# Modulation chunks multiplied as they land, cached key tiles spread over the first four tiles, spatial weights and norm tables loaded later

## The chip, the cores and the metric

The kernel runs on one core of one Trainium2 chip. The metric is device time in microseconds, the median of three runs. TensorE (PE) multiplies and transposes, VectorE (DVE) and ScalarE (ACT) compute on rows, GpSimd (POOL) does small reciprocal roots here, SyncE (SP) and ScalarE issue DMA transfers. All engines run their own instruction streams in order and meet at semaphores.

## The reference, cut to what matters

One encoder layer is computed for a prompt of 1024 tokens and for a sample of 64 tokens with 512 cached frames. The change touches only the first of its parts, the one that makes queries, keys, values and gates:

```python
mod = jax.nn.silu(c) @ w_ada + b_ada                     # 1024 -> 6*1024, for both conditionings
sh_a, sc_a, gt_a, sh_m, sc_m, gt_m = split(mod, 6)
h = rms_norm(x, g_norm_mix) * (1 + sc_a) + sh_a
proj = h @ w_in                                          # q latent 256, kv latent 128, rotary 32, u 512, v 512
q = rms_norm((rms_norm(q_lat) @ w_uq).heads)             # 8 heads of 96, then rotary
k, v = split(rms_norm(ckv_all) @ w_ukv)                  # ckv_all: 512 cached rows, then the new ones
k = rms_norm(concat(k_nope, krope)) , then rotary        # also for the 4 tiles of 128 cached rows
u = gelu(g_u); v_rows = layer_norm(gelu(g_v), g_ln_v, b_ln_v)
gm = u * (w_spatial @ v_rows + b_spatial)
```

Attention, the output projection and a mixture of 32 experts follow; they are the same in both kernels.

## The kernel before, in words

The first phase goes over nine tiles of tokens: the sample (64 rows) first, then the eight prompt tiles of 128 rows. Ahead of this loop stands a startup. It multiplies silu(c) by the first third of `w_ada`, which arrives as eight chunks of 1 MiB in a ring of three buffers (`ada_w`): SP issues chunk j once PE has multiplied chunk j-3 (`s_aused`). The remaining sixteen chunks come two per tile. From the eight products come the scale and shift columns (`adaT`, `modT`, `A1`), and from them the first tile's input `hT`, half written by DVE and half by ACT.

The startup also makes keys and values of three of the four tiles of cached rows (kt 9, 10, 11; kt 12 is made within the sample's tile). One such key tile is the function `kv`: two products with `W_ukv` on PE into two PSUM banks, squares and the copy of V on ACT, and on DVE the rotary turn, sums, a root from POOL (`rstd`), and the scaling into `kh`. ACT issues their stores to `v_scratch` and `k_scratch`; those of all later key tiles are issued by SP (`store_kv`). PE also transposes the spatial weights (`wsp`) in the startup. ACT issues the loads of `wsp`, `ln_g` and `ln_b` right after its first squares.

Each tile of the loop runs, on PE: the latent projection (`lat`, 416 columns), the key tile of the tile before (`kvs`), the projection `u`, transposes of the normed latents (`latT`) and of the next tile's normed x (`xT`), the spatial product of the tile before (`mix`), the projection `gv`, the queries (`W_uq`), and two chunks of `w_ada`. On DVE: norm of the latents (`latn`), norm of the next x (`xn`), the key tile (`kv`), `latT`, the next `hT`, `mix` of the tile before, layer norm of `gv`, norm and turn of the queries, and the scaling of one eighth of `W_out`.

Seven PSUM banks are handed out in rotation: the list `order1` names every use in the order of claims with its count of readers, and a use takes the next bank. PE claims a bank by waiting until all readers of its previous use are done (`bank_freed`). So the place of a use in the list decides on whom PE waits. POOL's roots and the halves of `kh`/`vh` (two buffers, in the order `key_order`) follow the same order.

## Time and profile before

| | us |
|---|---|
| median of 3 runs | 1124.41 (1123.81 to 1124.58) |
| profiled execution | 1130.84 |
| its span, first to last instruction | 1129.1 |
| PE busy in it | 1062.4 (94%) |
| DVE busy in it | 637.2 (56%) |
| ACT busy, POOL busy | 272.5 (24%), 306.3 (27%) |
| mean granted clock of PE | 0.958 |

The page of the profile gives busy times over the whole span; the first phase is only its first 304 us. In the first of its 40 slices of 28 us PE is busy to 3 tenths, in the second to 6, in the third to 8 and then 9 or more up to the tenth slice. The DMA engines are busy to 9, 8 and 9 tenths in the first three slices. So the startup is the one stretch of this phase in which PE stands idle much, and the rows below look into it and into the steady tiles behind it. In the timelines a row is: start in us, duration in us, engine, line, operation, output<-inputs, shape, number of instructions merged into it, and in brackets the idle time ahead of it with what ended it.

### The profile page before, as it was taken

The numbers are of one execution on the slowest core, as the hardware profiler recorded it, in microseconds if no ns is written. First come the engines' busy times: TensorE is split into PE (matmuls) and PEld (weight loads), VectorE is DVE, ScalarE is ACT, GpSimd is POOL, SyncE is SP. The second block draws the span as 40 slices with busy tenths as digits, with TensorE's granted clock in tenths as the row PEclk, the third lists the DMA queues.
The fourth block names the chain that finished last, engine by engine and source line by source line (L and its number), as shares of the span: only waits on it lengthen the run. The fifth ranks groups of instructions, "written<-read, shape, count | busy, mean of one in ns | idle before, by whom it ended". The sixth has DMA issues, their size and how long they took to land.

```text
span 1129.1 us, 14437 instructions
## 1 busy us (share of the span) xinstructions
PE 1062.4 (94%) x4921; PEld 703.6 (62%) x4921; DVE 637.2 (56%) x1280; ACT 272.5 (24%) x609; POOL 306.3 (27%) x350
## 2 busy tenths in 40 slices
PE   3689999999999899999999999899999999999994
PEld 0334555555556656676777775777777777777772
DVE  1455555555556556666766678546656454544443
ACT  1243222222332223223323211221111111111110
POOL 1222222222221011110101000224534544454554
PEclk9799999999957899999999999799999999999998
DMA  9894333333344143412403029669989999898950
GB/s 310 302 373 135 142 138 133 142 143 125 126 118 107 42 112 140 159 61 99 148 30 122 20 93 368 225 236 348 355 303 344 346 352 353 336 351 331 359 197 18
DMA packets 78102, 229.80 MB, mean 204 GB/s; under 512 B 29835, under 2 KB 33566, under 8 KB 62294
## 3 DMA queue, kind: packets, MB, share of 16 engines
q1 hardware_dynamic: 50608, 198.86, 47.3%
q0 software_dynamic: 24048, 26.81, 7.1%
q10 hardware_dynamic: 3382, 3.32, 0.9%
q8 instruction: 35, 0.57, 0.2%
q14 instruction: 29, 0.24, 0.1%
HBM read 201.23 MB, written 88.25 MB: 256 GB/s over the span
## 4 chain that ended last, share of the span: by engine, by line
PE 83%; DVE 9%; DMA 2%; issue 2%; ACT 2%; POOL 1%; ACTq 1%; DVEq 0%; SPq 0%; POOLq 0%
PE bank L1033 14%; PE bank L986 10%; PE bank L1392 10%; PE bank L1394 10%; PE bank L1409 10%; PE bank L1201 9%; PE bank L1146 7%; PE bank L1171 5%; PE bank L1114 2%; PE bank L1014 2%; PE bank L998 2%; PE bank L1044 1%; DMA grope<-in_g_knorm 1%; PE bank L1223 1%; POOL st L833 1%
## 5 line engine op out<-in xcount | busy, mean ns | idle before, releaser
L1033 PE MATMUL bank<-W_in,hT 128*128 128x512 f32 (+3 forms) x480 | 172.4, 540 | 3.8 <-DMA W_in<-in_w_in 3.8
L832 POOL TENSOR_SCALAR st<-st 128x1 f32<-128x1 f32 (+5 forms) x76 | 17.5, 230 | 565.6 <-DVEq L1767 268.6
L1033 PEld LDWEIGHTS bank<-W_in,hT 128*128 128x128 f32 (+1 forms) x480 | 80.0, 185 | 91.0 <-issue 87.9
L1409 PE MATMUL bank<-WD,hidT 128*128 128x512 f32 x264 | 119.0, 594 | 1.7 <-DVE hidT L2415 1.7
L1392 PE MATMUL bank<-WG,xT 128*128 128x256 f32 x528 | 119.5, 380 | 1.0 <-DVE xT L2399 1.0
L1394 PE MATMUL bank<-WU,xT 128*128 128x256 f32 x528 | 119.4, 380 | 0.0
L1201 PE MATMUL bank<-W_out,mT 128*128 128x512 f32 (+1 forms) x288 | 114.5, 561 | 0.1
L1394 PEld LDWEIGHTS bank<-WU,xT 128*128 128x128 f32 x528 | 100.5, 190 | 13.4
L1392 PEld LDWEIGHTS bank<-WG,xT 128*128 128x128 f32 x528 | 97.9, 190 | 13.0 <-issue 1.2
L1146 PE MATMUL bank<-kT,qT 104*128 104x512 f32 (+4 forms) x224 | 92.0, 528 | 0.7 <-ACTq L1647 0.6
L1171 PEld LDWEIGHTS bank<-vall,probT 128*128 128x128 f32 (+1 forms) x656 | 79.8, 191 | 18.8 <-issue 17.3
L2188 DVE COPY probT<-bank 128x512 f32<-128x512 f32 (+3 forms) x104 | 56.9, 547 | 59.5 <-PE bank L986 52.1
L2430 DVE TENSOR_TENSOR yb<-bank,gate_w 128x512 f32<-128x512 f32 x64 | 41.2, 686 | 77.4 <-PE bank L1409 77.4
L1171 PE MATMUL bank<-vall,probT 128*128 128x64 f32 (+1 forms) x656 | 83.1, 274 | 1.0 <-DVEq L1767 1.0
L1409 PEld LDWEIGHTS bank<-WD,hidT 128*128 128x128 f32 x264 | 47.7, 190 | 49.4 <-issue 47.3
L1201 PEld LDWEIGHTS bank<-W_out,mT 128*128 128x128 f32 (+1 forms) x288 | 46.5, 183 | 46.1 <-issue 40.3
L2407 DVE TENSOR_TENSOR hid<-sg,bank 128x256 f32<-128x256 f32 x33 | 20.1, 608 | 95.2 <-ACT sg L1722 95.2
L1729 ACT ACTIVATE gate_w<-gate_m,roww 128x1024 f32<-128x1024 f32 x33 | 37.9, 1151 | 139.5 <-DVE yb L2430 135.3
L833 POOL TENSOR_TENSOR st<-st,mhalf 128x1 f32<-128x1 f32 (+5 forms) x76 | 69.4, 914 | 6.3
L904 POOL DMA_INDIRECT residual_scratch<-acc,ids x32 | 41.1, 1284 | 69.9 <-DVE acc L2436 53.0
L907 POOL DMA_INDIRECT out<-acc,ids x33 | 38.3, 1159 | 72.2 <-DMA out<-acc,ids 64.5
L1146 PEld LDWEIGHTS bank<-kT,qT 104*128 104x128 f32 (+1 forms) x224 | 38.5, 200 | 28.1 <-issue 26.4
(330 smaller groups left out, 1474.5 us busy)
## 6 DMA issues: line engine op xcount, KB each, us to landing
WG<-in_w_gate_e SPq DMA_DIRECT2D x33, 1024.0 KB, 7.1
WU<-in_w_up_e SPq DMA_DIRECT2D x33, 1024.0 KB, 9.5
WD<-in_w_down_e SPq DMA_DIRECT2D x33, 1024.0 KB, 13.0
ada_w<-in_w_ada SPq DMA_DIRECT2D x24, 1024.0 KB, 7.8
residual_scratch<-x_att SPq DMA_DIRECT2D x32, 512.0 KB, 4.4
kbuf<-k_scratch SPq DMA_DIRECT2D x12, 384.0 KB, 5.1
xbuf<-in_x_prompt SPq DMA_DIRECT2D x8, 512.0 KB, 3.7
W_in<-in_w_in SPq DMA_DIRECT2D x2, 2048.0 KB, 22.6
```

The costliest lines, as they stand in the source:

```text
L833: g.tensor_tensor(dst, dst, mhalf[:dst.shape[0], 0:dst.shape[1]], ALU.pow).then_inc(s_rs, 1)
L904: g.indirect_dma_start(z_d[group], U(idx), acc[:, k], None, bounds_check=TOK - 1, oob_is_err=False).then_inc(s_zsc[group], 16)
L986: tr = lambda out, in_, r: nc.tensor.transpose(out, in_, ident[:r, :r])
L1033: ins = mm(out, hT[:, place_of[t] % 2, k, :R], W_in[:, k, c0 + c.start:c0 + c.stop], start=(k == 0), stop=(k == KD - 1))
L1146: ins = mm(out[:R, 0:m], qT[:depth, s % 2, h, :R], kT[:depth, h, k0 + c0:k0 + c0 + m], start=True, stop=True)
L1171: ins = mm(psum[7][:R, h * VD:(h + 1) * VD], probT[:r, u % 2, b, :R], vall[:r, slot0(t) + b, h * VD:(h + 1) * VD], start=(b == 0), stop=(b ...
L1201: ins = mm(out, (mT_last if s == LAST else mT)[:, k, :R], W_out[:, k, half * 512 + c.start:half * 512 + c.stop], start=(k == 0), stop=(k = ...
L1392: mm(psum[2][:, 0:DE], xT[:, k, :], WG[u][:, k, :], start=(k == 0), stop=(k == KD - 1))
L1394: ins = mm(psum[3][:, 0:DE], xT[:, k, :], WU[u][:, k, :], start=(k == 0), stop=(k == KD - 1))
L1409: ins = mm(psum[5 + half][:], hidT[:, k, :], WD[u][:, k, half * 512:(half + 1) * 512], start=(k == 0), stop=(k == 1))
L2188: ops.append(V.tensor_copy(probT[:, u % 2, 4 * j:4 * j + len(full), :R], src[:, 0:len(full), :R]))
L2430: V.tensor_tensor(y[:, c], psum[5 + half][:], gate_w[:, par, c], ALU.mult).then_inc(s_yv, 1)
```

## The change

In the startup PE takes chunks 0 to 5 of `w_ada` with only the transpose of the vectors among them; the rotary table product and the transposes of the cached latents stand behind chunk 5 instead of chunk 2, and the sample's x transposes stay behind chunk 6. No key tile is made in the startup. The four tiles of cached rows are made at the end of the first four tiles of the loop, one each (`late_kvs`), behind the queries and ahead of the two chunks of `w_ada` on PE, and behind the query turn and ahead of the `W_out` scaling on DVE. SP issues their stores, after the store of the queries. The spatial weights are transposed by PE at the end of the sample's tile, and DVE copies them behind the sample's queries. ACT issues `ln_g`, `ln_b` and `wsp` after it has written its half of the first `hT`. The bank rotation follows the new order.

```diff
     def kvs(i):
-        return ([9 + NC_ - 1] if i == 0 else [seq[i - 1]])
-    early_keys = list(range(9, 9 + NC_ - 1))
+        return [seq[i - 1]] if i else []
+    early_keys = []
+    def late_kvs(i):
+        return [9 + i] if i < NC_ else []
...
@@ SP, in the loop over tiles
             if i < LAST:
                 store_q(i)
+            for kt in late_kvs(i):
+                store_kv(sp, kt)
@@ PE, startup
-            if j == 2:
+            if j == 5:
                 pe.wait_ge(s_grope, 16 * 7)
...
-            if j == 3:
-                pe.wait_ge(s_cT, 1)
-                pe.wait_ge(s_fold1, 2)
-                for kt in early_keys:
-                    kv(kt)
-            if j == 5:
-                pe.wait_ge(s_wspl, 16)
-                for half in range(2):
...
@@ PE, in the loop over tiles, behind the queries
+            if i == 0:
+                pe.wait_ge(s_wspl, 16)
+                for half in range(2):
...
+            for kt in late_kvs(i):
+                kv(kt)
             if i < LAST:
                 for j in loop_ada(i):
                     ada(j)
@@ ACT, startup
-        act.dma_start(wsp[:], w["w_spatial"][0].rearrange("h t s -> t h s")).then_inc(s_wspl, 16)
+        ada(0)
+        hT_half(0)
         act.dma_start(ln_g[:], bcast(w["g_ln_v"], [P, GW])).then_inc(s_params, 16)
         act.dma_start(ln_b[:], bcast(w["b_ln_v"], [P, GW])).then_inc(s_params, 16)
-        for kt in early_keys[:-1]:
+        act.dma_start(wsp[:], w["w_spatial"][0].rearrange("h t s -> t h s")).then_inc(s_wspl, 16)
...
@@ DVE, in the loop over tiles
             turn(qh[:R, :, ND:], qh[:R, :, ND:], rope_q, t if t < NT else NC_, R, H)
             signal(s_qh)
+            if i == 0:
+                spatial_weights()
+            for kt in late_kvs(i):
+                kv(kt)
             if i:
                 k = i - 1
```

PE at the start of the program, before: `ada_w` are the chunks (4 products each), `grope` the rotary gains, `cn` the normed cached latents, `latT_c` their transposes.

```order
L998 MATMUL bank<-ada_w,c_act 2x512 x8
L986 MATMUL bank<-ident,vecs 128x85
L998 MATMUL bank<-ada_w,c_act 2x512 x4
L1058 MATMUL bank<-grope,ones 128x128
L986 MATMUL bank<-ident,cn 128x128 x4
L998 MATMUL bank<-ada_w,c_act 2x512 x4
L1014 MATMUL bank<-W_ukv,latT_c 128x512 x6
L998 MATMUL bank<-ada_w,c_act 2x512 x8
L986 MATMUL bank<-ident,wsp 128x128 x8
L998 MATMUL bank<-ada_w,c_act 2x512 x4
L986 MATMUL bank<-ident,xn 128x64 x8
L998 MATMUL bank<-ada_w,c_act 2x512 x4
```

And in the changed kernel (its line numbers are 14 higher here):

```order
L1012 MATMUL bank<-ada_w,c_act 2x512 x8
L1000 MATMUL bank<-ident,vecs 128x85
L1012 MATMUL bank<-ada_w,c_act 2x512 x16
L1072 MATMUL bank<-grope,ones 128x128
L1000 MATMUL bank<-ident,cn 128x128 x4
L1012 MATMUL bank<-ada_w,c_act 2x512 x4
L1000 MATMUL bank<-ident,xn 128x64 x8
L1012 MATMUL bank<-ada_w,c_act 2x512 x4
L1000 MATMUL bank<-ident,ada_row 128x98 x4
```

The three key tiles and the eight transposes of `wsp` are gone from between the chunks.

DVE between the queries of the second prompt tile and the latents of the third, before, with what each row waits for; `bank_freed` rows wait for DVE's own last read of a bank.

```order
L1839 TENSOR_TENSOR qh<-rot,rot_90 128x8x32 [waits dve_step]
L1990 TENSOR_SCALAR W_out<-W_out,vT 128x1024 [waits dve_step]
L1787 TENSOR_SCALAR latn<-lat,st 128x256 [waits dve_step,latent_square_sums_ready,reciprocal_roots_ready]
L1788 TENSOR_SCALAR latn<-lat,st 128x128 [waits dve_step]
L1815 TENSOR_SCALAR xn<-xbuf,st 128x1024 [waits dve_step,x_square_sum_ready,reciprocal_roots_ready]
```

In the changed kernel:

```order
L1853 TENSOR_TENSOR qh<-rot,rot_90 128x8x32 [waits dve_step]
L1849 TENSOR_TENSOR rot<-cck,rope_k 128x32 [waits dve_step]
L1852 TENSOR_TENSOR rot_90<-cck,rope_k 128x16 [waits dve_step] x2
L1853 TENSOR_TENSOR krot<-rot,rot_90 128x32 [waits dve_step]
L1866 ISA ctmp,st<-cck 128x32 [waits dve_step]
L1866 ISA st 128x1
L1868 TENSOR_REDUCE st<-sq_k 128x8 [waits k_squares_and_v_ready,dve_step]
L1869 TENSOR_SCALAR st<-st 128x8 [waits dve_step]
L1876 TENSOR_TENSOR kh<-bank,st 128x4x64 [waits dve_step,bank_filled0,stored_k0,reciprocal_roots_ready]
L1876 TENSOR_TENSOR kh<-bank,st 128x4x64 [waits bank_filled1,bank_freed0]
L1878 TENSOR_TENSOR kh<-krot,st 128x8x32 [waits bank_freed1]
L2009 TENSOR_SCALAR W_out<-W_out,vT 128x1024 [waits dve_step]
```

A whole key tile now stands ahead of `latn` on DVE; the tile's own key (`lat`, not `cck`) still follows `xn`, as before. The third place is PE's claim of a bank for `gv` in the second prompt tile. Before (`latT` without `_c` is the tile's own key):

```order
L1014 MATMUL bank<-W_ukv,latT 128x512 [waits bank_freed1]
L1014 MATMUL bank<-W_ukv,latT 128x512 [waits bank_freed2]
L1033 MATMUL bank<-W_in,hT 128x512 [waits bank_freed3]
L1033 MATMUL bank<-W_in,hT 128x512 x7
L986 MATMUL bank<-ident,latn 128x128 [waits bank_freed4,latents_normed]
...
L1044 MATMUL bank<-vrows,wspT 128x64 [waits bank_freed0,v_rows_ready]
L1044 MATMUL bank<-vrows,wspT 128x64 x7
L1033 MATMUL bank<-W_in,hT 128x512 [waits bank_freed1]
```

In the changed kernel:

```order
L1028 MATMUL bank<-W_ukv,latT 128x512 [waits bank_freed4]
L1028 MATMUL bank<-W_ukv,latT 128x512 [waits bank_freed5]
L1047 MATMUL bank<-W_in,hT 128x512 [waits bank_freed6]
L1047 MATMUL bank<-W_in,hT 128x512 x7
L1000 MATMUL bank<-ident,latn 128x128 [waits bank_freed0,latents_normed]
...
L1058 MATMUL bank<-vrows,wspT 128x64 [waits bank_freed3,v_rows_ready]
L1058 MATMUL bank<-vrows,wspT 128x64 x7
L1047 MATMUL bank<-W_in,hT 128x512 [waits bank_freed4]
```

The numbers of the banks moved, the relation did not: the last row, `gv`, takes the bank of the first half of the tile's own key tile (bank 1 before, bank 4 now), which DVE frees with its first `kh`.

## Rows read from the trace of the kernel before

**Rows 1.** Timeline of PE, startup and the first tiles.

```profile
24.31 0.79 PE L1058 MATMUL bank<-grope,ones 1*128 1x128 f32 x2 [3.89 <-DMA grope<-in_g_knorm]
28.45 6.64 PE L1014 MATMUL bank<-W_ukv,latT_c 128*128 128x512 f32 x12 [0.48 <-DVEq L1767]
...
36.85 1.09 PE L986 MATMUL bank<-ident,wsp 128*128 128x128 f32 x8
...
43.13 1.89 PE L998 MATMUL bank<-ada_w,c_act 128*2 128x512 f32 x8
...
50.46 5.19 PE L1033 MATMUL bank<-W_in,hT 128*64 128x208 f32 x32 [3.81 <-DMA W_in<-in_w_in]
...
64.69 3.67 PE L1033 MATMUL bank<-W_in,hT 128*64 128x256 f32 x32
71.31 2.26 PE L1114 MATMUL bank<-W_uq,latT 128*64 128x384 f32 x8 [2.95 <-DVEq L1767]
...
76.22 5.85 PE L1033 MATMUL bank<-W_in,hT 128*128 128x416 f32 x16
```

**Rows 2.** Stretches: busy us by engine, PE's granted clock, DMA share, GB/s.

```profile
0.00:25.00 25.00, 6.69 (x27) 1.00 (x27) 2.62 (x7) 4.26 (x12) 4.67 (x19) 1.00 0.92 307
25.00:40.00 15.00, 13.82 (x61) 5.13 (x60) 7.79 (x23) 2.53 (x8) 1.93 (x2) 1.00 0.64 220
40.00:65.00 25.00, 15.85 (x99) 9.28 (x101) 10.85 (x35) 9.61 (x25) 5.55 (x8) 0.73 1.03 390
72.00:75.00 3.00, 3.00 (x14) 0.50 (x14) 1.89 (x5) 0.97 (x2) 0.63 (x2) 0.50 1.03 410
```

**Rows 3.** Timeline of DVE, startup and the sample's tile.

```profile
47.64 1.48 DVE L1824 TENSOR_SCALAR hT<-bank,A,modT 128x64 f32<-128x64 f32 x4
49.70 1.42 DVE L1892 COPY wspT<-bank 128x512 f32<-128x512 f32 x2 [0.58 <-DVE hT L1824]
...
51.92 0.19 DVE L1835 TENSOR_TENSOR rot<-cck,rope_k 128x32 f32<-128x32 f32 x1
...
69.42 1.27 DVE L1900 TENSOR_SCALAR W_uq<-W_uq,vT 128x768 f32<-128x768 f32 x2
...
73.25 0.69 DVE L1961 BATCH_NORM_STATS2 st<-gv 64x6 f32<-64x512 f32 x1
...
84.95 0.35 DVE L1787 TENSOR_SCALAR latn<-lat,st 128x256 f32<-128x256 f32 x1 [1.65 <-POOL st L833]
```

**Rows 4.** Timeline of ACT, the copy of the sample's latents.

```profile
57.94 0.70 ACT L1580 ACTIVATE lat<-bank 64x208 f32<-64x208 f32 x2 [7.24 <-DVEq L1767]
```

**Rows 5.** Timeline of DVE, from one `gv` norm to the next.

```profile
128.83 0.69 DVE L1961 BATCH_NORM_STATS2 st<-gv 128x6 f32<-128x512 f32 x1 [1.45 <-ACTq L1613]
...
139.16 0.75 DVE L1990 TENSOR_SCALAR W_out<-W_out,vT 128x1024 f32<-128x1024 f32 x1
141.17 0.35 DVE L1787 TENSOR_SCALAR latn<-lat,st 128x256 f32<-128x256 f32 x1 [1.25 <-POOL st L833]
...
143.92 0.19 DVE L1835 TENSOR_TENSOR rot<-lat,rope_k 128x32 f32<-128x32 f32 x1
...
148.15 0.88 DVE L1862 TENSOR_TENSOR kh<-bank,st 128x256 f32<-128x256 f32 x2 [2.17 <-POOL st L833]
...
149.64 0.56 DVE L1948 COPY latT<-bank 128x384 f32<-128x384 f32 x1
```

**Rows 6.** Timeline of PE, prompt tiles: a key tile, and `gv` of the first four.

```profile
92.35 7.13 PE L1033 MATMUL bank<-W_in,hT 128*128 128x512 f32 x16
...
109.51 1.88 PE L1014 MATMUL bank<-W_ukv,latT 128*128 128x512 f32 x4
...
121.03 7.09 PE L1033 MATMUL bank<-W_in,hT 128*128 128x512 f32 x16
...
149.66 7.09 PE L1033 MATMUL bank<-W_in,hT 128*128 128x512 f32 x16
...
178.64 7.06 PE L1033 MATMUL bank<-W_in,hT 128*128 128x512 f32 x16
```

More of the change, by code:

```diff
@@ L684, in store_q @@
             sp.dma_start(q_d[P * t:P * t + R], qh[:R].rearrange("p h n -> p (h n)")).then_inc(s_out1["q"], 16)
+        for kt in early_keys:
+            store_kv(sp, kt)
         for i, t in enumerate(seq):
@@ L707, in _ @@
                 store_q(i)
+            for kt in late_kvs(i):
+                store_kv(sp, kt)
         nk = 0
@@ L1063, in _ @@
                 b1.full(ins, "cT")
-            if j == 3:
-                pe.wait_ge(s_cT, 1)
-                pe.wait_ge(s_fold1, 2)
-                for kt in early_keys:
-                    kv(kt)
-            if j == 5:
-                pe.wait_ge(s_wspl, 16)
-                for half in range(2):
-                    ps = b1.claim(pe, f"wsp{half}")
-                    for i in range(4):
-                        ins = tr(ps[:, i * P:(i + 1) * P], wsp[:, 4 * half + i, :], P)
-                    b1.full(ins, f"wsp{half}")
             if j == 6:
@@ L1078, in _ @@
         adaT(0)
+        pe.wait_ge(s_cT, 1)
+        pe.wait_ge(s_fold1, 2)
+        for kt in early_keys:
+            kv(kt)
         for i, t in enumerate(seq):
@@ L1116, in _ @@
                     b1.full(ins, (f"q{half}", t))
+            if i == 0:
+                pe.wait_ge(s_wspl, 16)
+                for half in range(2):
+                    ps = b1.claim(pe, f"wsp{half}")
+                    for j in range(4):
+                        ins = tr(ps[:, j * P:(j + 1) * P], wsp[:, 4 * half + j, :], P)
+                    b1.full(ins, f"wsp{half}")
+            for kt in late_kvs(i):
+                kv(kt)
             if i < LAST:
@@ L1621, in _ @@
             act.sem_inc(s_sqq, 1)
+            for kt in late_kvs(i):
+                kv(kt)
         nk = 0
@@ L1882, in _ @@
         signal(s_fold1)
-        for kt in early_keys[:-1]:
-            kv(kt)
         ada(0)
@@ L1889, in _, with spatial_weights @@
         hT_half(0)
-        for half in range(2):
-            ps = b1.read(dve, f"wsp{half}")
-            last_read(V.tensor_copy(wspT[:, 4 * half:4 * half + 4, :], ps[:].rearrange("p (h n) -> p h n", n=P)), f"wsp{half}")
-        do(V.memset(wspT[DEC:P, :, 0:DEC], 0.0))
-        signal(s_wsp)
-        kv(early_keys[-1])
+        for kt in early_keys:
+            kv(kt)
+        def spatial_weights():
+            for half in range(2):
+                ps = b1.read(dve, f"wsp{half}")
+                last_read(V.tensor_copy(wspT[:, 4 * half:4 * half + 4, :], ps[:].rearrange("p (h n) -> p h n", n=P)), f"wsp{half}")
+            do(V.memset(wspT[DEC:P, :, 0:DEC], 0.0))
+            signal(s_wsp)
         def late_constants():
@@ L1984, in _ @@
             signal(s_qh)
+            if i == 0:
+                spatial_weights()
+            for kt in late_kvs(i):
+                kv(kt)
             if i:
```

16 lines of the change are left out of this document (7 added, 9 removed).

## The prediction, made before the result was known

> **What bounds the kernel now.** I read the page first for the share of PE, then PE's timeline for the startup, the stretches for what DMA did meanwhile, and last the timelines of DVE and PE through a steady tile. The reader is to see two regimes. Up to 50.46 us PE mostly waits: it is busy 6.69 of the first 25 us while DMA moves 307 GB/s, busy for 13.82 of the next 15 while DMA falls to 220 GB/s, and its first big product starts at 50.46 when part of `W_in` lands [rows 1, 2]. That dip is what the key tiles cost: the chunk ring holds three buffers, PE does three key tiles in 6.64 us from 28.45 on, takes no chunk meanwhile, and SP issues none. From 40 to 65 us DMA is full at 390 GB/s. In the second regime, the prompt tiles, PE runs without a gap: `gv` starts at 92.35, 121.03, 149.66 and 178.64, 28.65 us apart, the last with 0.35 of modulation transposes ahead [rows 6].
>
> The second regime has a loop that nearly binds. `gv` takes the bank of the tile's own key, which DVE frees with its first `kh`. From `gv`'s start to DVE's norm of it is 7.8 us (121.03 to 128.83). From there to the scaling of `W_out` 10.3, to `latn` 2.0 (of it 1.25 for POOL's root), to the start of the tile's key 2.75 (143.92), to the end of its first `kh` 4.7 (148.15 plus half of 0.88), and 0.1 to PE: 27.65 in all, where PE takes 28.65 [rows 5, 6]. DVE is busy for 56% of the span, yet here it is 1.0 us from setting the pace, since the loop is made of waits on POOL, ACT and PE as much as of work.
>
> **The startup.** What has to have moved before chunk 5 is there: inputs of 1.1 MB, six chunks of 1.05 MB, the rotary table and vectors 0.3, in all 7.7 MB. At the first 25 us' 307 GB/s that is 25.0 us [rows 2]. If the loads that ACT no longer issues early (1.05 MB) gave nothing back it would be 2.7 us later at 390 GB/s, 27.7. I take the middle, 26.3. The rotary gains were there at 24.31 [rows 1]. Then PE has chunk 5 (1.9), the rotary product (0.8), four transposes (at most the 1.1 of eight), chunk 6 (1.9), eight small transposes (1.1) and chunk 7 (1.9), so it ends at 35.0 [rows 1]. From chunk 7's end to `hT` it was 45.02 to 49.12 [rows 1, 3], 4.1 us, so `hT` stands at 39.3 with the semaphore. Two chunks and the latent columns of `W_in` (3.8 MB) take 9.7 us from chunk 5 on and land at 36.0: PE no longer waits for them. The sample's first product starts at 39.3 instead of 50.46, 11 us earlier. The removed key tiles, transposes, waits and stores of the startup are thereby paid out; they aren't counted again.
>
> **The sample's tile.** Two paths lead to DVE's first norm of `gv`, at 73.25 before. By DMA: the rest of `W_in`, one x tile, `W_uq` and ACT's three moved loads are 6.55 MB, 16.8 us, so `W_uq` lands at 52.8 (51.6 if chunk 5 came at 25.0), and from DVE's scaling of `W_uq` to the norm it was 69.42 to 73.25, 3.8 us [rows 3]: 56.7 or 55.5. By PE: 39.3, the latent product 5.2 at half clock as before, from ACT's copy of the latents to `gv` 57.94 to 64.69, 6.75 [rows 1, 4], then `gv` 3.7 and about 1 for the gelu: 56.0. I take 56.3, which is 16.95 earlier than before. The bounds are 54.8 (chunk 5 at 25.0 and 410 GB/s, the rate of the stretch 72 to 75 [rows 2]) and 59.5 (chunk 5 at 27.7 and 370).
>
> Behind that norm DVE has the sample's queries as before, and now also the spatial weights, 49.70 to 51.92 or 2.2 us [rows 3], and the first late key, whose length is a key tile's from start to what follows it, 143.92 to 149.64, 5.7 us [rows 5]. Only then comes `latn` of the first prompt tile, which before had 0.4 of waiting more than a steady one (1.65 against 1.25 [rows 3, 5]). So `latn`, and with it that tile's key and `gv`, move by -16.95 - 0.4 + 2.2 + 5.7 = -9.45: `gv` at 82.9. PE is there earlier: its tile ends with the queries from 55.1 (2.3), `wsp` 1.1, the key 1.9 and two chunks 3.8, at 64.2, and 16.1 later, as from 76.22 to 92.35, it stands at `gv` at 80.3 [rows 1, 6]. It waits 2.6 us.
>
> **The next three tiles.** Each now has a late key in the DVE loop: 27.65 + 5.7 = 33.4 us. PE has 28.65 + 1.9 = 30.5 [rows 6], so DVE sets the pace and PE waits 2.9 us a tile. The fourth `gv` comes at 82.9 + 3 x 33.4 + 0.45 (that tile's modulation transposes, or DVE's second `kh`) = 183.5, where it was 178.64. This is 4.9 us later. From there no late key is left, the loop is 27.65 again, PE is the bound and keeps the delay; nothing later depends on absolute time. The cover that hid each early key on DVE was the wait for DMA; in the loop its cover is the 1.0 of slack, spent before the first of the three.
>
> The stores move to SP behind the store of the queries. Behind them on SP wait the next x tile and two chunks; they are issued up to 5.7 us later than before, and PE uses the chunks only at the end of a tile of 33 us, so I cost them at nothing. ACT's late work (two squares, two copies) lies in its wait for the next latents, at nothing as well. If a chunk came late at the end of a tile, each tile would add the excess.
>
> **The clock.** After PE's wait ahead of 71.31 (2.95 us) the granted clock was 0.50, the 1.2 GHz level, from 72 to 75 [rows 1, 2]; 3 us at half speed lose 1.5 us of PE work. The changed kernel has four waits of 2.6 to 2.9 us, and what follows each is `gv`, which is in the loop. So the bounds are 0 and 4 x 1.5 = 6.0; the nearest row is one slightly longer wait, and it did drop the clock. I take one drop, 1.5, since these waits are shorter. The Trainium skill has a rule that speaks against this change (TensorE: Matmul & The Clock Gate, section What's actually happening): throttled is the default and activity releases it. By the trace alone one wait of this length is followed by half clock; by the rule every one may be, which is the last rival's 6.0 instead of 1.5. The trace agrees with the rule in its one case (0.50 after 2.95 us idle).
>
> **The sum.** -11.2 at the first product, -9.45 at the first prompt tile's `gv`, +4.9 at the fourth, +6.4 with one drop of the clock. The profiled execution has a span of 1129.1, so its span would be 1135.5 and its time of 1130.84 would be 1137.2. It runs 6.4 us above the median of 1124.41; the difference carries over to the median unchanged: 1130.8.
>
> **Rivals.** *Not slower: the late keys are hidden.* If DVE's key ran within slack, PE alone would set the pace: the first prompt tile starts 12.0 us earlier (64.2 for 76.22) and three keys at 1.9 cost 5.7, which gives -6.3 and 1118.1. For it speaks DVE's 56%, against it the 1.0 us of slack. It decides at a DVE cost per late key of 1.0 + 1.9 = 2.9 us; 5.7 is measured. The same side would be reached if the norm at 56.3 came before 51.4, which the 18 MB forbid at 390 GB/s.
>
> *The loads come back.* The loads of ACT stand in one stream with `W_in` and `W_uq`, and small packets may slow it; then the norm is at 59.5, the change costs 8.1 without the clock and some 9.6 with one drop: 1134.0. For it: DMA had nothing to spare from 40 us on. Against it: stores of 2 MB left the same stretch.
>
> *The clock falls at each wait.* 4.9 + 6.0 = +10.9, 1135.3.
>
> *The change doesn't do what it says.* The rotary gains arrive on ACT's queue, and with SP's chunks now without gaps they may be later than 24.31. PE would then stand behind chunk 5 as it stood behind chunk 2. From 28.2 on each us late costs one; 4 us late gives 1134.8.
>
> **How the numbers follow.** Forecast case, none to two drops and loads as worked out (3.4 to 7.9 slower): 0.60. Clock at each wait: 0.12. Loads or gains late: 0.14. Keys hidden: 0.07. Something near no change, a better start with a cheaper key: 0.07, of which 0.04 within 0.2%, what a measurement of this kernel can tell from none (2.2 us), 0.01 below and 0.02 above. Faster 0.08, same 0.04, slower 0.88. The range goes from +2.1, a little under the lowest start, to +11.1: 1126.5 to 1135.5, with 0.1 left out on each side at most.
>
> **What would show it.** Right: the first product of `W_in` near 39; no DMA dip between 25 and 40 us; DVE's first norm of `gv` near 56; `gv` of the first four prompt tiles 33.4 us apart with PE idle some 2.9 us ahead of each, ended by DVE's `kh`; 28.65 apart from the fourth on. Wrong: `gv` 30.5 apart, which would mean that DVE's key costs less in the loop than in the row; a first product later than 43, which would put the fault into the startup; or PE waiting for chunks at the end of a tile, which would put it on SP.

## The result, and the profile after

The changed kernel is slower: median 1143.89 us of four executions (1135.54 to 1144.66) against 1124.34 (1123.81 to 1124.58), ratio 1.0157 with a 95% interval of 1.0121 to 1.0192. The forecast was 1130.8, in a range of 1126.5 to 1135.5. The direction was right and the time lies 8.4 us above the upper end. The same kernel was measured twice more later (below): 1134.18 against 1125.00, and 1139.96 against 1124.55. The loss is therefore 9 to 20 us by the medians, and the first measurement is the highest of the three.

The timeline of PE after, from the startup to the fourth prompt tile's `gv`. Columns are those of [rows 1]; the `W_in` product is line 1047 here, the key tile line 1028.

```profile
28.43 0.79 PE L1072 MATMUL bank<-grope,ones 1*128 1x128 f32 x2
...
38.93 9.22 PE L1047 MATMUL bank<-W_in,hT 128*64 128x208 f32 x64 [2.90 <-ACTq L1562]
...
58.92 1.88 PE L1028 MATMUL bank<-W_ukv,latT_c 128*128 128x512 f32 x4
...
62.56 5.85 PE L1047 MATMUL bank<-W_in,hT 128*128 128x416 f32 x16
...
84.39 8.83 PE L1047 MATMUL bank<-W_in,hT 128*128 128x512 f32 x16 [2.50 <-DVE kh L1876]
...
119.45 8.83 PE L1047 MATMUL bank<-W_in,hT 128*128 128x512 f32 x16 [1.91 <-DVE kh L1876]
...
154.50 10.13 PE L1047 MATMUL bank<-W_in,hT 128*128 128x512 f32 x16 [1.92 <-DVE kh L1876]
...
191.12 0.74 PE L1000 MATMUL bank<-ident,ada_row 98*128 98x98 f32 x4 [2.19 <-DVE kh L1876]
191.66 8.57 PE L1047 MATMUL bank<-W_in,hT 128*128 128x512 f32 x16
```

Three things are to be seen. The startup is 11.5 us shorter: the first product of `W_in` stands at 38.93 instead of 50.46 [rows 1]. The first prompt tile's `gv` keeps 8.0 of that (84.39 for 92.35 [rows 6]). Then the four `gv` are 35.06, 35.05 and 37.16 apart where they were 28.7, each behind a wait for DVE's `kh` (the fourth behind the transposes of `ada_row`, which take that wait), and each takes 8.6 to 10.1 us where it took 7.1 [rows 6].

The stretches of the same kernel, columns as in [rows 2]:

```profile
0.00:25.00 25.00, 9.03 (x41) 0.72 (x41) 2.62 (x7) 4.26 (x12) 4.67 (x19) 1.00 0.91 308
25.00:40.00 15.00, 10.43 (x53) 3.69 (x50) 4.89 (x12) 2.21 (x5) 0.00 (x0) 0.92 1.03 394
...
85.50:88.50 3.00, 3.00 (x5) 1.08 (x4) 2.59 (x6) 0.00 (x0) 0.00 (x0) 0.50 0.30 69
```

The DMA dip between 25 and 40 us (220 GB/s in [rows 2]) is gone: 394 GB/s. The last row explains the 8.83: at the beginning of `gv` the granted clock is 0.50, the 1.2 GHz level. The other three `gv` show 0.51 or 0.52 in the same place.

The timeline of DVE, the sample's tile and the first loop (line 1915 scales `W_uq`, 1976 is the norm of `gv`, 2009 scales `W_out`, 1801 makes `latn`):

```profile
53.83 1.27 DVE L1915 TENSOR_SCALAR W_uq<-W_uq,vT 128x768 f32<-128x768 f32 x2 [3.51 <-DMA W_uq<-in_w_uq]
...
57.68 0.69 DVE L1976 BATCH_NORM_STATS2 st<-gv 64x6 f32<-64x512 f32 x1 [0.17 <-ACTq L1625]
...
77.01 0.35 DVE L1801 TENSOR_SCALAR latn<-lat,st 128x256 f32<-128x256 f32 x1 [1.33 <-POOL st L845]
...
93.93 0.69 DVE L1976 BATCH_NORM_STATS2 st<-gv 128x6 f32<-128x512 f32 x1 [2.28 <-ACTq L1625]
...
104.27 0.19 DVE L1849 TENSOR_TENSOR rot<-cck,rope_k 128x32 f32<-128x32 f32 x1
...
109.99 0.75 DVE L2009 TENSOR_SCALAR W_out<-W_out,vT 128x1024 f32<-128x1024 f32 x1
111.98 0.35 DVE L1801 TENSOR_SCALAR latn<-lat,st 128x256 f32<-128x256 f32 x1 [1.24 <-POOL st L845]
...
118.97 0.88 DVE L1876 TENSOR_TENSOR kh<-bank,st 128x256 f32<-128x256 f32 x2 [2.17 <-POOL st L845]
```

A late key takes DVE 104.27 to 109.99, 5.72 us. From `gv`'s start to its norm it is 9.54 (84.39 to 93.93) instead of the 7.8 before: the slower `gv` lies inside the loop, and DVE waits 2.28 for it.

The chain that ended last, by engine, was PE 83%, DVE 9%, POOL 1% before. After:

```profile
PE 77%; DVE 12%; POOL 3%; issue 3%; DMA 2%; ACT 2%; SPq 0%; DVEq 0%; ACTq 0%; POOLq 0%
```

Busy times of the whole span tell nothing of all this: DVE is busy 56% in both.

### The profile page after: what moved, and what is told of

The parts are those of the page before. It is cut to its first block, busy times and chain, and to the rows that moved or that the text cites. A ratio compares the mean times of both kernels' runs of the same rounds, so it can differ in the third digit from the quotient of the medians.

```text
span 1142.8 us, 14434 instructions
## 1 busy us (share of the span) xinstructions
PE 1070.6 (94%) x4921; PEld 705.7 (62%) x4921; DVE 637.1 (56%) x1280; ACT 272.9 (24%) x609; POOL 305.1 (27%) x350
## 4 chain that ended last, share of the span: by engine, by line
PE 77%; DVE 12%; POOL 3%; issue 3%; DMA 2%; ACT 2%; SPq 0%; DVEq 0%; ACTq 0%; POOLq 0%
PE bank L1047 11%; PE bank L1407 10%; PE bank L1000 10%; PE bank L1409 10%; PE bank L1424 10%; PE bank L1216 9%; PE bank L1161 6%; PE bank L1186 5%; POOL st L845 3%; DMA ada_w<-in_w_ada 2%; PE bank L1012 1%; PE bank L1120 1%; PE bank L1238 1%; PE bank L1058 1%; PE bank L1028 1%
## 5 line engine op out<-in xcount | busy, mean ns | idle before, releaser
L1047 PE MATMUL bank<-W_in,hT 128*128 128x512 f32 (+3 forms) x480 | 182.3, 569 | 9.2 <-DVE kh L1876 6.3
L1047 PEld LDWEIGHTS bank<-W_in,hT 128*128 128x128 f32 (+1 forms) x480 | 84.2, 195 | 102.0 <-issue 91.6
L1407 PE MATMUL bank<-WG,xT 128*128 128x256 f32 x528 | 121.9, 385 | 1.0 <-DVE xT L2418 1.0
L1161 PE MATMUL bank<-kT,qT 104*128 104x512 f32 (+4 forms) x224 | 88.9, 512 | 0.7 <-ACTq L1661 0.6
L921 POOL DMA_INDIRECT out<-acc,ids x33 | 36.0, 1091 | 67.8 <-DMA out<-acc,ids 59.0
## 6 DMA issues: line engine op xcount, KB each, us to landing
WD<-in_w_down_e SPq DMA_DIRECT2D x33, 1024.0 KB, 13.1
```

The source lines that it names most:

```text
L1047: ins = mm(out, hT[:, place_of[t] % 2, k, :R], W_in[:, k, c0 + c.start:c0 + c.stop], start=(k == 0), stop=(k == KD - 1))
L1161: ins = mm(out[:R, 0:m], qT[:depth, s % 2, h, :R], kT[:depth, h, k0 + c0:k0 + c0 + m], start=True, stop=True)
L1407: mm(psum[2][:, 0:DE], xT[:, k, :], WG[u][:, k, :], start=(k == 0), stop=(k == KD - 1))
```

## The experiments

All in which no other kernel is named are edits of the changed kernel. Four groups ran; within one, kernels shared a chip and the runs of the kernel before, whose medians were 1127.04, 1124.96, 1125.00 and 1124.55. Several expectations name 1144, the changed kernel's first median; the median of all its executions turned out to be 1139.5 (below), and times are compared with that.

**The clock: keep PE busy ahead of `gv`.** The spatial product is repeated, so that PE works where it waited.

```diff
+            for again in range(3 if i == 0 else 2 if i < NC_ else 1):
                 for h in range(H):
                     ins = mm(ps[:R, h * 64:(h + 1) * 64], wspT[:R, h, :R], ...
```

> The changed kernel, with PE doing the spatial product of the four tiles that have a late key behind them twice over (three times for the sample's) into the same bank, about 1.9 us of repeated work right ahead of each gv, where PE waits anyway. Theory (DVE sets the pace at 33.4 us a tile and each wait of PE is followed by half clock, which stretches gv in the loop): gv starts 33.4 us apart instead of 35.06, 35.05 and 37.2, gv takes 7.1 instead of 8.8 to 10.1, granted clock 1.0 from 70 to 195 us, the fourth prompt tile's gv near 184 instead of 191.7, and the kernel 7 to 8 us faster than the changed one, near 1136. Rival (the clock costs nothing because PE is not the bound there, the excess is DVE's): the intervals stay at 35, the time stays at 1144 or grows by up to 2.

Measured: 1135.35 (1130.15 to 1139.35) against 1127.04, ratio 1.0082 (1.0052 to 1.0112). PE of its profile:

```profile
83.25 7.13 PE L1047 MATMUL bank<-W_in,hT 128*128 128x512 f32 x16 [0.64 <-DVE kh L1877]
...
116.60 7.13 PE L1047 MATMUL bank<-W_in,hT 128*128 128x512 f32 x16
...
149.99 7.13 PE L1047 MATMUL bank<-W_in,hT 128*128 128x512 f32 x16
...
184.00 7.13 PE L1047 MATMUL bank<-W_in,hT 128*128 128x512 f32 x16
```

The first two distances are 33.35 and 33.39, every `gv` takes 7.13, and the granted clock from 60 to 200 us is 1.00. So the DVE loop was worked out rightly (33.4), and what lies above it in the changed kernel goes with the clock: more work on PE made PE faster where it counts. By the fourth `gv` (184.00) this kernel is 6.0 us behind the kernel before (178.64 and 177.38), the changed kernel in its three profiles 11.8 on average (below): about half of the loss is the DVE loop, and half the clock. The time is 4.2 below the changed kernel's 1139.5, where 7 to 8 were expected. It does not show this alone, since its interval overlaps with that of the changed kernel's first repetition (1.0061 to 1.0135); the timeline does.

**The bank: let `gv` take the latents' bank.** A fixed assignment of banks in the prompt tiles, so that `gv` does not stand behind the tile's own key.

```diff
+        if i:
+            places |= {("lat", t): 0, ("gv", t): 0, ("q0", t): 1, ("q1", t): 2, ("u", t): 3, ("mix", seq[i - 1]): 3, ("latT", t): 4}
+            places |= {("kv0", seq[i - 1]): 1, ("kv1", seq[i - 1]): 2, ...
```

> The changed kernel with another assignment of PSUM banks in the prompt tiles: gv takes the bank of the latents, which ACT frees early, and no longer that of the tile's own key. Theory (DVE's own chain is as long as the loop): the wait moves from gv to the transposes of latn and xn, the tiles stay 33 to 35 us apart, the time is within 3 us of the changed kernel's 1144. Rival (the claim of the bank is the fault): 30.5 us a tile, PE without waits, 1130 or less.

Measured: 1139.29 (1130.61 to 1143.50), ratio 1.0104 (1.0069 to 1.0139). PE:

```profile
68.79 7.35 PE L1057 MATMUL bank<-W_in,hT 128*128 128x416 f32 x16 [6.09 <-DVE wspT L1918]
...
117.70 7.08 PE L1057 MATMUL bank<-W_in,hT 128*128 128x512 f32 x16
...
146.16 0.55 PE L1010 MATMUL bank<-ident,latn 128*128 128x128 f32 x3 [0.89 <-DVEq L1791]
148.10 1.09 PE L1010 MATMUL bank<-ident,xn 128*128 128x128 f32 x8 [1.39 <-DVEq L1791]
```

`gv` no longer waits, but the transposes of `latn` and `xn` ahead of it do, and from the second to the third `gv` it is 33.06 us (117.70 to 150.76). DVE's `latn` stands at 79.02, 112.31, 145.38 and 178.44, 33.1 to 33.3 apart throughout. The bank was only where the wait appeared; the chain through `latn` on DVE sets the pace. The experiment isn't clean. My assignment put the first prompt tile's latents behind the copy of `wspT`, 6.09 us that the changed kernel doesn't have; with PE that late, the second `gv` stands only 31.28 behind the first. In the fourth tile the clock falls behind waits of 0.89 and 1.39, and the transposes of `ada_row` wait 1.36 for DVE's `latT`, whose bank I gave them: the fourth `gv` stands 37.72 behind the third. The time is within 0.3 us of the changed kernel's 1139.5.

**The price: late keys without sums and root.** The cached keys are scaled by a constant column; their sums of squares and POOL's root are left out.

```diff
+            sc = vT[:, R_BSP:R_BSP + 8] if kt >= 9 else st[:, 32:40]
-            do(V.tensor_reduce(st[:R, 32:40], sq_k[:R], AXX, ALU.add))
-            ...
-            rstd()
+            if kt < 9:
+                ... (the same three)
```

> The changed kernel without the sums and the root of the four cached key tiles (their keys are scaled by another column, so that part of the result is not computed). A late key is then 2.5 us on DVE instead of 5.7, under the 2.9 us at which PE's own 30.5 us a tile become the bound. Theory (threshold): the first prompt tile's gv near 81, then 30.5 us apart without a wait ahead of gv and without a fall of the clock behind it, the fourth near 173, the time near 1125, 19 us below the changed kernel. Rival (no threshold, each us of DVE counts as one): 4 x 3.2 = 13 us, 1131.

Measured: 1120.70 (1116.00 to 1124.38), ratio 0.9942 (0.9920 to 0.9965). PE:

```profile
83.50 7.13 PE L1045 MATMUL bank<-W_in,hT 128*128 128x512 f32 x16 [2.48 <-DVE kh L1876]
...
113.90 7.09 PE L1045 MATMUL bank<-W_in,hT 128*128 128x512 f32 x16
...
144.25 7.08 PE L1045 MATMUL bank<-W_in,hT 128*128 128x512 f32 x16
```

The distances are 30.40 and 30.35, near PE's own 28.65 + 1.9, and no wait is left ahead of the second and third. A late key takes DVE 2.59 us here (101.68 to 104.27). With DVE's price under the threshold of 2.9 us the change is a gain. The first `gv` came at 83.50 where I expected 81: in this profile PE waited 1.04 for `W_in` and `W_uq` landed at 55.14, neither of which the edit touches. Here a wait of 2.48 was not followed by half clock, so the expectation of no fall held although that wait was there.

**One half of the change: late keys with the old startup.** The chunk order, the loads and the place of the `wsp` transposes are as before; only the keys are late.

```diff
-            if j == 5:
+            if j == 2:
                 pe.wait_ge(s_grope, 16 * 7)
...
-            if i == 0:
-                spatial_weights()
```

> The kernel before with the four cached key tiles late, but with the order of the chunks and of the rotary table, the transposes and loads of the spatial weights and the loads of the norm tables where they were. Theory: taking the key tiles out gives most of the startup's gain already; the rotary table still holds chunk 3 until 26, so the first product of W_in starts near 42 instead of 38.9, DVE has the 2.2 us of spatial weights off its loop, so the first prompt tile's gv is within 2 us of the changed kernel's 84.4, and the time within 4 us of 1144. Rival (the order of the chunks makes the startup's gain): first product near 46 to 50, gv near 90, and a time of 1150 or more.

Measured: 1138.58 (1135.14 to 1143.22), ratio 1.0115 (1.0086 to 1.0144). PE:

```profile
42.37 4.73 PE L1045 MATMUL bank<-W_in,hT 128*64 128x208 f32 x32 [2.90 <-ACTq L1560]
...
84.27 10.08 PE L1045 MATMUL bank<-W_in,hT 128*128 128x512 f32 x16 [1.13 <-DVE kh L1874]
...
120.59 8.83 PE L1045 MATMUL bank<-W_in,hT 128*128 128x512 f32 x16 [1.92 <-DVE kh L1874]
```

The first product is 3.4 us later than with the new chunk order, and the first prompt tile's `gv` stands at the same place (84.27 for 84.39). So 8.1 of the 11.5 us at the first product come from taking the keys away. The other 3.4, of the chunk order, don't reach `gv`: they are 2.1 at DVE's norm of the sample's `gv` (59.75 for 57.68), and behind it the changed kernel loses those, since its DVE makes `wspT` behind the sample's queries (67.89 to 70.10, 2.2 us), which this variant does at 42.09. The first prompt tile's `latn` is at 76.88 here and at 77.01 in the changed kernel. The time is 0.9 below the 1139.5.

**The other half: the new startup, no late keys.** kt 9 to 11 are made behind the transposes of `ada_row`, kt 12 in the sample's tile.

```diff
     def kvs(i):
-        return [seq[i - 1]] if i else []
-    early_keys = []
+        return [seq[i - 1]] if i else [12]
+    early_keys = [9, 10, 11]
     def late_kvs(i):
-        return [9 + i] if i < NC_ else []
+        return []
```

> The other half of the change by itself: the chunk order, the rotary product and cn transposes behind chunk 5, the loads and the wsp transposes late as in the changed kernel, but no late keys: kt 9, 10 and 11 are made in the startup behind adaT, kt 12 in the sample's tile as before. Nothing is left out. Theory: PE has 5.7 us of keys in a stretch that DMA bounds; DVE has 17 us of them from about 36 on, with hT ahead of them, and its W_uq scaling, due at 53.8, comes at 55 to 57 instead; the first gv norm at 58 to 62, the spatial weights behind it, gv of the first prompt tile at 80 to 84 (92.35 before the change), and from there 28.7 apart with no half clock. The time is 8 to 12 us below the kernel before the change: 1115 to 1119 by a median of 1127 for that. Rival (the startup on DVE and its clock eat the gain): first gv at 88 or later, 1 to 4 us below before.

Measured: 1128.74 (1122.89 to 1137.01) against 1124.96, ratio 1.0042 (1.0018 to 1.0065). It is slower than before, and both my cases had it faster; only the rival's late `gv` (88 or later) came, at 93.85. PE:

```profile
50.07 5.26 PE L1047 MATMUL bank<-W_in,hT 128*64 128x256 f32 x32 [4.10 <-DVE kh L1876]
61.35 0.58 PE L1000 MATMUL bank<-ident,latn 64*128 64x64 f32 x3 [6.02 <-DVEq L1781]
...
93.85 8.83 PE L1047 MATMUL bank<-W_in,hT 128*128 128x512 f32 x16 [2.41 <-DVE kh L1876]
```

I had counted the keys on DVE as hidden by the wait for `W_uq`. But the sample's latents are on PE long before, and DVE reaches their `latn` only at 60.58, behind three keys (47.74 in the changed kernel). The kernel before had two of the three ahead of `hT` (DVE 28.40 to 43.39), and its first product still waited for `W_in` and not for them; behind `hT` DVE is the path. So neither half is a gain alone, and the whole isn't either. This variant is not exactly what is left of the change without its late keys, since all three keys stand behind `hT`, where neither kernel has them.

**The loads of ACT.** `wsp`, `ln_g` and `ln_b` are issued early again.

```diff
+        act.dma_start(wsp[:], w["w_spatial"][0]...
+        ... (ln_g and ln_b)
         ada(0)
         hT_half(0)
-        ... (ln_g and ln_b)
-        act.dma_start(wsp[:], w["w_spatial"][0]...
```

> The changed kernel with ACT issuing wsp, ln_g and ln_b right after its first squares again, as before. Nothing else changes. Theory of the prediction (1.05 MB of loads moved behind hT give the chunks 1.4 to 2.7 us, but the same bytes come back ahead of W_uq): the first W_in product starts 1 to 2.5 us later than 38.9, W_uq lands within 1 us of 53.8, and the time is within 3 us of the changed kernel's. Rival (the later loads help the gv of the first prompt tile): gv starts 1.5 to 3 us later than 84.4 and the time is 2 to 4 us above the changed kernel's. A third outcome, W_uq earlier and the time lower by over 1 us, would say that the moved loads in one stream with W_in and W_uq cost what the second rival of the prediction held.

Measured: 1137.88 (1135.91 to 1145.48), ratio 1.0128 (1.0096 to 1.0160). DVE:

```profile
53.51 1.27 DVE L1915 TENSOR_SCALAR W_uq<-W_uq,vT 128x768 f32<-128x768 f32 x2 [3.26 <-DMA W_uq<-in_w_uq]
```

`W_uq` is scaled at 53.51, within the changed kernel's own three profiles (53.83, 53.62, 52.78); the first product is at 39.13, 0.2 later where I expected 1 to 2.5; `gv` is at 84.05. The time is 1.6 below the changed kernel's 1139.5, inside what one kernel spreads. No effect of the moved loads shows either way.

**The changed kernel twice more, and the kernel before as a subject.**

> The changed kernel itself once more, word for word, for how far its time spreads and whether its waits come each time. Theory (the clock falls behind each of the four waits, and 13 us of span are lost by the fourth gv): the same four intervals near 35.05, 35.05 and 37.2 in its profile, within 1.7 for each; over its executions the time falls as the mean granted clock rises, from about 1144.5 at 0.956 to about 1135.5 at 0.966, and the median is 12 to 18 us above the median of the kernel before in the same call. Rival (the 19.5 us between the two medians is what the change costs, and the profiled execution of before was merely slow): 17 to 21 us.

> The changed kernel a third time, for the size of its loss. It was 19.5 us above the median of the kernel before in the first measurement (four executions) and 9.2 in the second (six). Theory (the mechanism costs a fixed part, about 10 to 13 us by the fourth gv; the rest of the 19.5 came of executions with a lower granted clock after 300 us, where the two kernels are the same): 9 to 13 us above before, and in its profile gv intervals of 34.3 to 37.2 in the first four tiles. Rival (it costs 19.5 and the second measurement was the odd one): 16 to 21 us.

> The kernel before, word for word, timed like the others against itself. Theory: its executions spread over 9 to 13 us with the mean granted clock (0.960 to 0.977), the median within 1.5 us of that of the comparison's own runs of before, so that a difference between two kernels read from single executions is uncertain by some 5 us; its profile shows no half clock between 80 and 300 us, as in the first profile, and gv 28.65 apart. Rival (the first profile, at 0.958 and 1130.84, is typical): the median of its executions lies above 1128.

Measured: 1134.18 (1132.23 to 1140.40), ratio 1.0098 (1.0061 to 1.0135); 1139.96 (1130.80 to 1144.06), ratio 1.0130 (1.0089 to 1.0170); the kernel before 1124.68 (1116.57 to 1128.65), ratio 0.9997 (0.9975 to 1.0020). Its profile, at 1127.23, shows a granted clock of 1.00 from 85 to 300 us like the first one; the rival, a median above 1128, is out. PE of the changed kernel, in the profile of the first repetition, and of the second:

```profile
84.70 9.44 PE L1047 MATMUL bank<-W_in,hT 128*128 128x512 f32 x16 [0.80 <-DVE kh L1876]
...
120.40 8.66 PE L1047 MATMUL bank<-W_in,hT 128*128 128x512 f32 x16 [1.92 <-DVE kh L1876]
...
155.31 7.13 PE L1047 MATMUL bank<-W_in,hT 128*128 128x512 f32 x16 [1.92 <-DVE kh L1876]
...
189.65 9.81 PE L1047 MATMUL bank<-W_in,hT 128*128 128x512 f32 x16
```

```profile
83.52 8.83 PE L1047 MATMUL bank<-W_in,hT 128*128 128x512 f32 x16 [2.50 <-DVE kh L1876]
...
118.59 8.82 PE L1047 MATMUL bank<-W_in,hT 128*128 128x512 f32 x16 [1.92 <-DVE kh L1876]
...
153.64 7.13 PE L1047 MATMUL bank<-W_in,hT 128*128 128x512 f32 x16 [1.91 <-DVE kh L1876]
```

From the second `gv` on the waits come each time to a hundredth; whether the clock falls behind one does not. In the first repetition the first fall stands ahead of `gv`: PE had waited 1.31 for `latn` and 1.39 for `xn`, its transposes of `xn` took 1.97 instead of 1.09, and only 0.80 of wait was left. The fourth `gv` is at 191.66, 189.65 and 187.97 in the three profiles, and at 178.64 and 177.38 in the two of before. Behind it before takes 950.5 and 948.1 us to the end of the span, the changed kernel 951.1, 946.9 and 950.5: on average 949.5 and 949.3, so nothing is lost or won later. By the profiles the mean loss is therefore 12.0 us of span (1139.3 for 1127.3), of it 11.8 by the fourth `gv`. All 16 executions of the changed kernel have a median of 1139.5, some 15 above before. The distances of `gv` were expected within 1.7 of the first profile's; the last of the first repetition is 34.34 for 37.2 and misses that. Of the medians, the first repetition, 9.2, came out under both cases of its expectation, and the second, 15.4, between theory (9 to 13) and rival (16 to 21). Where the 3 us between profiles and medians lie stays open.

**The cure: hide POOL's root of the late key.** The key's turn and sums are done while POOL takes the queries' root, its scaling after the queries' turn. Nothing is left out.

```diff
-            rstd()
+            if late_kvs(i):
+                dve.sem_inc(s_ms, 1)
+                kv(late_kvs(i)[0], 0)
+            rstd(signalled=bool(late_kvs(i)))
...
-                kv(kt)
+                rstd(signalled=True)
+                kv(kt, 1)
```

> The changed kernel with its four late keys woven into the queries' turn on DVE: the key's rotary turn and sums are done while POOL takes the queries' root, and its scaling into kh comes once the queries are turned, so that POOL's key root passes under DVE work. Nothing is left out. Theory (a late key costs its DVE length in the loop; above 2.9 us of it DVE sets the pace, PE waits 2 to 2.5 us ahead of each gv and the clock falls behind each wait): I reckon 1.0 to 2.5 us added to the DVE loop for a late key instead of 5.7, so 27.65 + 2.5 = 30.2 at most against PE's 30.5; the last three gv intervals are 30.4 to 30.7 as they were without sums and root (30.4), gv takes 7.1 and no half clock stands between 60 and 300 us; time 12 to 20 us below the changed kernel, 1118 to 1124. Rival (the cost of a late key is not the wait on POOL's root but its DVE instructions and its bank on PE): the intervals stay above 32 and the time within 5 us of the run that did the spatial product twice (1135), 1130 to 1138.

Measured: 1119.19 (1112.38 to 1121.38) against 1124.96, ratio 0.9932 (0.9908 to 0.9956). PE, then DVE:

```profile
81.89 7.13 PE L1047 MATMUL bank<-W_in,hT 128*128 128x512 f32 x16 [1.73 <-DVE kh L1883]
...
112.29 7.09 PE L1047 MATMUL bank<-W_in,hT 128*128 128x512 f32 x16
...
142.64 7.09 PE L1047 MATMUL bank<-W_in,hT 128*128 128x512 f32 x16
```

```profile
97.50 1.15 DVE L2006 TENSOR_TENSOR qh<-bank,st 128x384 f32<-128x384 f32 x2 [0.25 <-DVE st L1871]
...
100.47 0.88 DVE L1883 TENSOR_TENSOR kh<-bank,st 128x256 f32<-128x256 f32 x2 [0.24 <-DVE qh L1853]
```

In the changed kernel the queries' scaling waits 2.18 for POOL and the late `kh` another 2.18; the waits are now 0.25 and 0.24, the rest filled with the key's turn and sums and with the queries' turn. The key costs DVE about 1.9 instead of 5.7 (from the norm of `gv` to `W_out` it is 12.2 us, where it was 10.3 before and 16.1 in the changed kernel), the loop is under PE's 30.5, the distances are 30.40 and 30.35, and the clock stays up. This is some 20 us below the median of all executions of the changed kernel, without taking an instruction away.

**Where the late keys stand.** Four variants of that cure: two early keys, one early key, none early but the late ones in the prompt tiles 1 to 4 instead of the sample's tile and 1 to 3, and one early with the others in prompt tiles 1 to 3. The edit of the last:

```diff
-    early_keys = []
+    early_keys = [9]
     def late_kvs(i):
-        return [9 + i] if i < NC_ else []
+        return [9 + i] if 1 <= i <= NC_ - 1 else []
```

> The same, with two of the four cached key tiles back in the startup, but behind the last chunk and the adaT transposes, where PE and DVE wait for W_in; the other two stay late, in tiles 1 and 2 of the loop order (the sample and the first prompt tile). Nothing is left out. Theory: PE has 3.8 us less work in the stretch in which it is the bound, and the startup has room, since PE ends its chunks at 35 and the sample's products are bound by W_in and by the clock until 57: 3 to 4 us below the kernel with all four late and overlapped, 1114 to 1120. Rival (the startup has no room: DVE has 11.4 us of keys ahead of the sample's norms): DVE's W_uq scaling or norm of gv comes up to 4 us later, the gain is taken back and it is within 1 us of all four late.

> The kernel with overlapped late keys, with one cached key tile behind the adaT transposes in the startup and three late. Nothing is left out. With two early the norm of the sample's gv came at 62.86 and its latn transposes waited 6.1 us for DVE; with none early gv's norm was near 59. Theory (DVE, 6 us for a key ahead of the sample's latn, is the path of the startup; about 4 us of it is hidden by the wait for W_in): one early key costs 0 to 2 us at the norm and saves PE 1.9, so gv of the first prompt tile at 81 to 83.5 and the time within 2 us of no key early (1119.2 by 1125.0 for before), 1117 to 1121. Rival (any key ahead of latn delays it by its whole length): gv at 84 or later and 1121 to 1124.

> The kernel with overlapped late keys, but with the four in the four prompt tiles behind the sample's instead of in the sample's and the three behind it. Nothing is left out. Theory: the last wait ahead of a prompt tile's gv (1.73 at 81.89) comes of the key and the spatial weights that stand between the sample's queries and the first latn on DVE; without the key, latn is about 1.7 us earlier and PE 1.9 earlier too, so gv is at 80 with 1.5 to 2 us of wait left or less, the four intervals are 30.4, and the fifth gv is 0 to 1.8 us earlier than with the sample's tile used: 1117 to 1120 by 1125 for before. Rival (PE and DVE both only shift): within 0.5 us of it.

> Overlapped late keys, one cached key tile behind the adaT transposes in the startup, and the other three in the three prompt tiles behind the sample's (none in the sample's tile). Nothing is left out. It joins two versions: with one early and the late ones in the sample's and the next two tiles gv of the first prompt tile was at 80.64 after a wait of 1.53 for DVE; with none early and the sample's tile free of a key it was at 78.75 after 1.15. Theory: gv at 78.5 to 80.5, three intervals of 30.4 behind it instead of four, so 1.5 to 2 us below either: 1115.5 to 1118 by 1125 for before. Rival (the early key delays DVE's latn by what PE saves): 1118 to 1120.

Measured, in this order: 1121.58 (1114.17 to 1126.28) against 1124.96, ratio 0.9962 (0.9932 to 0.9992); 1118.06 (1114.19 to 1121.18) against 1125.00, 0.9950 (0.9928 to 0.9973); 1119.16 (1110.47 to 1124.07) against 1125.00, 0.9955 (0.9929 to 0.9982); 1115.87 (1110.39 to 1124.71) against 1124.55, 0.9943 (0.9910 to 0.9976). Their intervals overlap with each other and with the plain cure: which is best can't be told from these runs, that each beats the kernel before can. What tells them apart is PE's timeline. With two early keys:

```profile
38.40 3.03 PE L1047 MATMUL bank<-W_in,hT 128*64 128x208 f32 x32
...
53.52 0.58 PE L1000 MATMUL bank<-ident,latn 64*128 64x64 f32 x3 [6.13 <-DVEq L1781]
...
85.70 8.83 PE L1047 MATMUL bank<-W_in,hT 128*128 128x512 f32 x16 [1.76 <-DVE kh L1883]
```

With one early key and three in tiles 1 to 3:

```profile
39.12 3.03 PE L1047 MATMUL bank<-W_in,hT 128*64 128x208 f32 x32 [1.00 <-ACTq L1562]
...
79.68 7.13 PE L1047 MATMUL bank<-W_in,hT 128*128 128x512 f32 x16
```

Two early keys hold `latn` back (52.75, against 47.74 in the changed kernel) and with it the norm of `gv` (62.86), as the rival of that expectation had it; its median is 2.4 above the plain cure, where the rival allowed 1, and above the 1114 to 1120 of the theory. The other three medians lie inside their forecasts. For tiles 1 to 4 the rival, no difference to the plain cure, fits as well (1119.16 and 1119.19). One early key fits: `gv` is at 79.68 with no wait ahead of it at all, and the three behind it follow at 30.40, 30.35 and 30.69. It also fills PE's wait for `hT` (1.00 left of 2.90), and the product behind it takes 3.03 where it takes 4.7 to 5.5 behind a wait of 2.90.

## Why the prediction was right in direction and wrong in size

*The startup: right.* First product forecast 39.3, measured 38.93, with no DMA dip. The rival of late rotary gains is out: that product ran at 28.43 without a wait.

*The sample's tile: right within 1.7.* DVE's first norm was forecast at 56.3 and is at 57.68, of it 1.0 from `W_uq` (53.83 for 52.8), and at 57.97 and 56.79 in the repetitions. The first prompt tile's `gv` carries that over: 82.9 forecast, 84.39, 84.70 and 83.52 measured. PE's side was read wrongly, without consequence: the 3.8 for two chunks takes rows at half clock (1.89 each), they took 1.90 together, and PE then waited 1.30 for `latn` and 1.39 for `xn`, waits that the prediction doesn't have. The rival of returning loads had 59.5 and is out, and the last loads don't matter.

*The DVE loop: right.* 33.4 us a tile, measured at 33.35 and 33.39 once the clock was kept up; the late key costs 5.72 for 5.7. The threshold of 2.9 us was not tried closely, but the runs lie as it says: at 5.7 a loss, at 2.6 (without the root) and at 1.9 a gain. The rival of hidden keys fails only on this price.

*The clock: this is the step that failed.* It said "I take one drop, 1.5, since these waits are shorter". The waits ahead of `gv` were in fact shorter still, 0.80 to 2.50, since 0.66 to 0.69 of the 2.9 came ahead of the `xn` transposes in all tiles but the first. Yet four of four `gv` in the first profile, and three of four in each repetition, ran at half clock for a part. These ten grew by 1.1 (8.20) to 3.0 (10.13), six of them by 1.4 to 1.7, where the term had one growth of 1.5. In the first profile the distances exceed 33.4 by 1.66, 1.65 and 3.3 (37.16 less the 0.45 of `ada_row`), 6.6 in all, and the fourth `gv` lasts 1.5 longer: 8.1 for the 1.5 forecast. The same sum gives 7.0 and 4.9 in the repetitions, 6.7 on average. The reason given, shorter waits, had no row behind it: going from the one wait that was followed by half clock to one drop in four waits was a guess. The trace of before even held a second such wait that I did not count (3.21 ahead of 42.52, and 0.50 granted behind it). The rival "the clock falls at each wait" had the mechanism, with a chance of 0.12, and its 6.0 is near the average. The Trainium skill (TensorE: Matmul & The Clock Gate, section What's actually happening) has throttled as the default, which activity releases; here the trace agrees for 10 of the 12 `gv` in the three profiles, not for all.

*The change of base: wrong too.* It said that the 6.4 us by which the profiled execution stood above its median carry over unchanged. They don't. Of the 91 later executions of the kernel before, the longest took 1130.06: that profile was at the far end of its own spread. The three profiles of the changed kernel stand 0.8, 4.1 and 0.3 above their medians. Forecast for the profiled execution was 1137.2, and the three took 1144.66, 1138.29 and 1140.27, on average 3.9 more. The median of all 16 executions exceeds 1130.8 by 8.7; 3.9 of it is this, and 4.8 came in with the base (6.4 subtracted where 1.6 was due). Of the 13.1 by which the first measurement missed, 7.5 are its profiled execution (1144.66 for 1137.2) and 5.7 the base. Read as a difference between the two kernels, the forecast was +6.4 and the spans of the profiles gave +12.0; the sample's tile (1.3) and the clock (6.7 for 1.5) cover that within 1 us. The medians give 3 more, and three of the first four executions were granted 0.955 or 0.956, lower than most of the later twelve (0.954 to 0.972). Why is open.

## What to carry to other kernels

A loop through two engines has a slack that can be added up from the starts of a steady tile; an added piece is free only up to it, however idle either engine looks. Where two fifths of the piece are a wait for a third engine (2.18 of 5.72 here), weave it into work that already waits for that engine before deciding where to put it. And price each new wait of TensorE in a loop with a fall of its clock behind it, in a range from none to all, with the median of several executions as the base.

## What the runs showed of the hardware that was not expected

Waits of 1.91 to 2.19 us ahead of the second to fourth prompt tile's `gv`, equal to a hundredth from run to run, were followed by the 1.2 GHz level in 11 of 15 cases (three profiles of the changed kernel, one each of the late keys alone and the early loads). Ahead of the first prompt tile's `gv`, where the clock was still full, waits of 1.76, 2.41 and 2.50 were, and 0.64, 1.15, 1.53, 1.73 and 2.48 were not. Length alone doesn't decide it, nor does the sum of the pauses since the last big product: with the spatial product repeated, 1.44, 1.39 and 0.64 were not followed by it. The kernel before shows the same without any edit. Its PE waits 3.21 us for DVE ahead of the sample's second four `xn` transposes in the first profile and 3.22 in the second:

```profile
42.52 0.69 PE L986 MATMUL bank<-ident,xn 64*128 64x64 f32 x4 [3.21 <-DVE kh L1862]
```

```profile
42.32 0.46 PE L986 MATMUL bank<-ident,xn 64*128 64x64 f32 x4 [3.22 <-DVE kh L1862]
42.72 1.04 PE L998 MATMUL bank<-ada_w,c_act 128*2 128x512 f32 x8
```

Behind the first the granted clock is 0.50, and the chunk takes 1.89 [rows 1]; behind the second it is 1.00, and the chunk takes 1.04. What decides stays open.

One kernel on one core spreads over more than 1%: the kernel before took 1116.18 us at a mean granted clock of 0.977 and 1129.48 at 0.961. Much of it arises where both kernels are the same: of the 6.3 us between the spans of the first two profiles of the changed kernel 4.3 come behind the fourth `gv`, and the stretch from 300 to 420 us was granted 0.84 in the one and 0.93 in the other (0.84 in the third).
